# Expert products as plain float32 calls on quarters of the matmul array, in jobs of 96 row slots

## The reference

```python
def moe_swiglu(x, router, w1, w3, w2):
    xt = x.reshape(-1, d)
    logits = (xt @ router).astype(F32)
    top_v, top_i = lax.top_k(logits, TOP_K)          # 2 of 8
    gates = jax.nn.softmax(top_v, axis=-1)
    combine = jnp.sum(jax.nn.one_hot(top_i, N_EXPERTS) * gates[..., None], axis=1)
    for e in range(N_EXPERTS):
        out = out + combine[:, e:e + 1] * swiglu(xt, w1[e], w3[e], w2[e])

def swiglu(x, w1, w3, w2):
    return (jax.nn.silu(x @ w1) * (x @ w3)) @ w2     # 1024 -> 3584 -> 1024
```

## Time and profile before

| | |
|---|---|
| time, median of 3 runs (lowest, highest) | 1520.54 us (1519.48, 1522.57) |
| span of the profiled execution, first to last instruction | 1517.9 us |
| TensorE busy | 1491.3 us, 98% |
| TensorE weight loads busy (beside the products) | 1298.2 us, 86% |
| VectorE, ScalarE busy | 1237.9 us (82%), 962.7 us (63%) |
| bytes read from memory, written | 446.45 MB, 36.87 MB |
| expert stage, first product of the first job to the last product of the last | from 541.95 to about 1503.9 us |

### The profile page before, as it was taken

How to read it: one execution, slowest core, us unless ns; L and a number is a source line. 1 busy time by engine, 2 the same in 40 slices (tenths; PEclk the granted TensorE clock), 3 DMA queues, 4 the chain that set the end, 5 groups by cost and what they waited for, 6 DMA issues and landing times.

```text
span 1517.9 us, 23455 instructions
## 1 busy us (share of the span) xinstructions
PE 1491.3 (98%) x8803; PEld 1298.2 (86%) x8804; DVE 1237.9 (82%) x906; ACT 962.7 (63%) x693; POOL 82.7 (5%) x65
## 2 busy tenths in 40 slices
PE   9998999999999999999999999999999999999997
PEld 9987899999999878888888888888888888888885
DVE  6898865655578788889888888888888888888887
ACT  6634443333353577777777777777777777777774
POOL 1035100000000120000000000000000000000300
PEclk9999999999999999999999999999999999999999
DMA  9644788888555679999999999999999999999991
GB/s 318 214 135 151 268 304 297 298 306 310 188 191 174 225 257 393 395 369 384 373 365 390 368 379 373 369 389 370 374 382 370 373 384 358 387 376 369 387 396 45
DMA packets 212938, 483.97 MB, mean 319 GB/s; under 512 B 8810, under 2 KB 26314, under 8 KB 209820
## 3 DMA queue, kind: packets, MB, share of 16 engines
q1 hardware_dynamic: 209224, 473.67, 85.9%
q10 hardware_dynamic: 2388, 5.32, 0.9%
q0 software_dynamic: 1280, 4.33, 0.7%
HBM read 446.45 MB, written 36.87 MB: 318 GB/s over the span
## 4 chain that ended last, share of the span: by engine, by line
PE 87%; DVE 1%; issue 0%; ACT 0%; DVEq 0%
PE Q L2544 20%; PE Q L2495 14%; PE Q L2497 14%; PE Q L2496 14%; PE Q L2039 7%; PE Q L2040 7%; PE Q L2041 7%; PE Q L2528 2%; DVE wlo L1174 1%; PE Q L2474 0%; PE Q L2505 0%; ACT yrows L1149 0%; PE Q L2400 0%; PE Q L2408 0%; PE Q L2032 0%
## 5 line engine op out<-in xcount | busy, mean ns | idle before, releaser
L1174 DVE TENSOR_TENSOR wlo<-raw,whi 128x2048 fp32r<-128x2048 f32 x413 | 940.6, 2295 | 197.9 <-ACT whi L988 120.1
L988 ACT ACTIVATE whi<-raw 128x2048 fp32r<-128x2048 f32 x336 | 642.9, 1921 | 179.3 <-PE Q L2497 84.1
L2495 PE MATMUL Q<-whi,xgh 128*128 128x512 f32 x896 | 358.0, 400 | 0.0
L2497 PE MATMUL Q<-whi,xgl 128*128 128x512 f32 x896 | 352.9, 394 | 0.0
L2496 PE MATMUL Q<-wlo,xgh 128*128 128x512 f32 x896 | 352.2, 393 | 0.0
L2039 PE MATMUL Q<-xh,whi 128*128 128x264 f32 x1024 | 293.7, 287 | 5.0 <-DVEq L1285 1.8
L2040 PE MATMUL Q<-xl,whi 128*128 128x264 f32 x1024 | 291.2, 284 | 0.0
L2041 PE MATMUL Q<-xh,wlo 128*128 128x264 f32 x1024 | 289.8, 283 | 0.0
L2497 PEld LDWEIGHTS Q<-whi,xgl 128*128 128x128 f32 x896 | 168.7, 188 | 39.3
L2496 PEld LDWEIGHTS Q<-wlo,xgh 128*128 128x128 f32 x896 | 168.7, 188 | 36.5
L2495 PEld LDWEIGHTS Q<-whi,xgh 128*128 128x128 f32 x896 | 168.9, 189 | 35.5
(11 more groups left out here) (286 smaller groups left out, 1140.4 us busy)
## 6 DMA issues: line engine op xcount, KB each, us to landing
raw<-in_moe_w SPq DMA_DIRECT2D x336, 1024.0 KB, 7.6
raw<-in_ffn_w SPq DMA_DIRECT2D x42, 1024.0 KB, 7.5
raw<-in_hgrn_w_in SPq DMA_DIRECT2D x16, 1024.0 KB, 7.3
xg_rows<-zeros SPq DMA_DIRECT2D x6, 2048.0 KB, 10.9
y_rows<-zeros SPq DMA_DIRECT2D x6, 2048.0 KB, 11.5
raw<-in_conv_w_in SPq DMA_DIRECT2D x12, 1024.0 KB, 5.5
raw<-in_hgrn_w_out SPq DMA_DIRECT2D x4, 1024.0 KB, 5.2
raw<-in_conv_w_out SPq DMA_DIRECT2D x4, 1024.0 KB, 5.0
```

The lines of the kernel that those rows point to most:

```text
L988: a.activation(bufs(q)[0], raw[:, n % RAW, PW * (q % 2):PW * (q % 2 + 1)], ACT.Copy).then_inc(hi_done, 1)
L1174: v.tensor_tensor(low, raw[:, slot, PW * half:PW * (half + 1)], high.bitcast(F32), ALU.subtract).then_inc(lo_done, 1)
L2495: t_.matmul(out, xgh[:, kt, :], high[:, w], start=(kt == 0), stop=False)
L2497: mm = t_.matmul(out, xgl[:, kt, :], high[:, w], start=False, stop=(kt == DT - 1))
```

## The change

In the expert stage nothing is split any more. The weights go from memory into a ring of six pieces of 1 MiB (`ring`) and TensorE reads them there; the rows (`xgt`), the turned hidden rows (`ht`) and the weights are plain float32. A job has 96 row slots (`SLOT`), three groups of 32. In `up_m` each slice of the inputs takes six calls with 32 columns of weights: for each group one call over the first 384 of the 512 hidden columns, with its output on that group's own partitions, and then for each group one call over the last 128 columns, all three on partitions 96 to 127. In `down_m` each 128 hidden columns take twelve calls of 256 columns, four at a time on the four quarters of the partitions. A block has 48 + 48 + 48 calls instead of 24 + 24 + 24. `turn` has three transposes. The splits, `hi_m`, `lo_m`, `early`, `hth`/`htl`, `xgh`/`xgl` go away. Five pieces of the first job are loaded during the convolution and one after the routing's last use of that place; every later piece waits until the piece six before it is used. In the last job the result leaves PSUM in five pieces instead of two. The zero fill is 96/128 of its bytes. A few semaphores are merged (`a_mm`, `turned`, `tok_ready`).

```diff
-SPLIT_M = 6
-AHEAD_M = SPLIT_M - 1
+RING = 6
+SLOT = 96
+GROUP = 32
+MAIN = 384
+TAIL = P
+YW = 256
...
-    SLOTS = 3 * P
+    SLOTS = 3 * SLOT
+    GROUPS = SLOT // GROUP
+    PIECES = 2 * JOB
...
+        def y_tail(n):
+            return Q[1][SLOT:P, n // 2, YW * (n % 2):YW * (n % 2 + 1)]
...
+            def load_piece(q, src):
+                slot = q % RING
+                sp.dma_start(ring[:, slot, :].rearrange("p (k w) -> p k w", k=src.shape[1]), src
+                             ).then_inc(piece_loaded[slot], 16)
...
             for c in range(6):
                 chunk(C_CIN + c, kp(conv_w_in[0])[:, :, FW * n:FW * (n + 1)])
+                if c == 3:
+                    sp.wait_ge(sem("squares_summed"), len(NORMS))
+                    for slot in range(4):
+                        sp.wait_ge(sem(f"state_out{slot}"), 16 * SLOT_OF.count(slot))
+                    sp.wait_ge(sem("prompt_state_out"), 32)
+                if c >= 3:
+                    early_piece(c - 3)
             for c in range(2):
                 chunk(C_COUT + c, kp(conv_w_out[0])[:, :, FW * c:FW * (c + 1)])
+                early_piece(3 + c)
+            sp.wait_ge(sem("xs_gained"), TT)
+            sp.wait_ge(sem("xs_ready"), TT)
+            early_piece(5)
+
+            def pair(k, q, src, reg=None):
+                for half in range(2):
+                    free = k * PIECES + (2 * C_MOE + q + half - RING + 1)
+                    sp.wait_ge(used, free if reg is None else free + reg * 6)
+                    n = src.shape[1] // 2
+                    load_piece(q + half, src[:, n * half:n * (half + 1), :])
...
-            early(0)
-            early(1)
-            early(2)
...
-                a.activation(hs[:, :], Q[0][:, 0, :], ACT.Silu).then_inc(sem("hs_ready"), 1)
+                a.activation(hs[:, :], Q[0][:, 0, 0:MAIN], ACT.Silu).then_inc(sem("hs_ready"), 1)
...
-                    for j in range(2):
-                        act.wait_ge(sem("y_mm"), j + 1)
-                        a.activation(yh[:, 512 * j:512 * (j + 1)], Q[1][:, j, :], ACT.Copy
-                                     ).then_inc(sem("yh_ready"), 1)
+                    act.wait_ge(sem("y_mm"), 1)
+                    a.activation(yh[0:SLOT, 0:2 * YW], Q[1][0:SLOT, 0, :], ACT.Copy).then_inc(sem("yh_ready"), 1)
+                    act.wait_ge(sem("y_mm"), 2)
+                    a.activation(yh[0:SLOT, 2 * YW:3 * YW], Q[1][0:SLOT, 1, 0:YW], ACT.Copy)
+                    for n in range(GROUPS):
+                        ins = a.activation(yh[GROUP * n:GROUP * (n + 1), 3 * YW:D], y_tail(n), ACT.Copy)
...
-                        mm = t_.matmul(Q[0][:, 2 + half, P * (d % 4):P * (d % 4 + 1)],
-                                       xs[0:r, t, P * d:P * (d + 1)], pm[0:r, t, :],
+                        mm = t_.matmul(Q[0][:, 2 + half, P * (d % 4):P * (d % 4) + SLOT],
+                                       xs[0:r, t, P * d:P * (d + 1)], pm[0:r, t, 0:SLOT],
...
             def piece(k, q, reg):
-                w = k * (2 * JOB) + (M0 + q + 1)
-                pe.wait_ge(lo_done, w if reg is None else w + reg * 6)
+                n = k * FB + (q // RING + 1)
+                pe.wait_ge(piece_loaded[q % RING], (n if reg is None else n + reg) * 16)
+                return ring[:, q % RING, :]

             def up_m(bank, k, q, reg, first=False):
+                out = Q[0][:, bank, :]
                 for half in range(2):
...
                     for c in range(4):
                         kt = 4 * half + c
-                        w = slice(FW * c, FW * (c + 1))
-                        out = Q[0][:, bank, :]
-                        t_.matmul(out, xgh[:, kt, :], high[:, w], start=(kt == 0), stop=False)
-                        t_.matmul(out, xgh[:, kt, :], low[:, w], start=False, stop=False)
-                        mm = t_.matmul(out, xgl[:, kt, :], high[:, w], start=False,
-                                       stop=(kt == DT - 1))
+                        for n in range(GROUPS):
+                            g_ = slice(GROUP * n, GROUP * (n + 1))
+                            t_.matmul(out[g_, 0:MAIN], xgt[:, kt, g_], w[:, FW * c:FW * c + MAIN],
+                                      start=(kt == 0), stop=(kt == DT - 1), skip_group_check=True)
+                        for n in range(GROUPS):
+                            g_ = slice(GROUP * n, GROUP * (n + 1))
+                            mm = t_.matmul(out[SLOT:P, TAIL * n:TAIL * (n + 1)], xgt[:, kt, g_],
+                                           w[:, FW * c + MAIN:FW * (c + 1)], start=(kt == 0 and n == 0),
+                                           stop=(kt == DT - 1), skip_group_check=True)
                     mm.then_inc(used, 1)
...
-                        for c, j in ([(0, 0), (1, 0), (0, 1), (1, 1)] if by_bank else
-                                     [(0, 0), (0, 1), (1, 0), (1, 1)]):
+                        for cb, c in (itertools.product(range(GROUPS), range(2)) if by_bank else
+                                      [(cb, c) for c in range(2) for cb in range(GROUPS)]):
+                            f = 2 * half + c
+                            bank, col = cb // 2, YW * (cb % 2)
                             for n in range(GROUPS):
+                                mm = t_.matmul(Q[1][GROUP * n:GROUP * (n + 1), bank, col:col + YW],
+                                               rows_of_h(ht, f, n), w[:, D * c + YW * cb:D * c + YW * (cb + 1)],
+                                               start=start, stop=(last and f == 3), skip_group_check=True)
+                            mm = t_.matmul(Q[1][SLOT:P, bank, col:col + YW], rows_of_h(ht, f, cb),
+                                           w[:, D * c + 3 * YW:D * (c + 1)],
+                                           start=start, stop=(last and f == 3), skip_group_check=True)
```

More of the change, by code:

```diff
@@ L11 @@
+import itertools
 from contextlib import ExitStack
@@ L290, in build @@
         raw_loaded = [[sem(f"raw_loaded{i}_{half}") for half in range(2)] for i in range(RAW)]
+        piece_loaded = [sem(f"piece_loaded{i}") for i in range(RING)]
         hi_done, lo_done, used = sem("hi_done"), sem("lo_done"), sem("pieces_used")
@@ L472, in body @@
             def body(k, e, row, ahead):
[L474 to L480, removed]
+                with sp.Fori(0, FB - 2) as i:
+                    pair(k, 6, tiles_of(moe_w3, e, 0, DT)[:, :, bass.ds(i * FW + FW, FW)], i)
+                    pair(k, 8, tiles_of(moe_w2, e, i * 4, 4), i)
+                    pair(k, 10, tiles_of(moe_w1, e, 0, DT)[:, :, bass.ds(i * FW + 2 * FW, FW)], i)
@@ L976, in _ @@
             M0 = 2 * C_MOE
-            def hi_m(k, q0, q1, reg=None):
-                for q in range(q0, q1):
-                    n = q // 2
-                    loads = k * (JOB // RAW) + (n // RAW + C_MOE // RAW + 1)
-                    free = k * (2 * JOB) + (M0 + q - SPLIT_M + 1)
-                    if reg is not None:
-                        loads, free = loads + reg, free + reg * 6
-                    act.wait_ge(raw_loaded[n % RAW][q % 2], loads * 16)
-                    act.wait_ge(used, free)
-                    a.activation(bufs(q)[0], raw[:, n % RAW, PW * (q % 2):PW * (q % 2 + 1)],
-                                 ACT.Copy).then_inc(hi_done, 1)
-            def early(q):
-                if MOE_SLOT[q] < SPLIT:
-                    act.wait_ge(used, M0 + MOE_SLOT[q] - SPLIT + 1)
-                hi_m(0, q, q + 1)
-            early(0)
-            early(1)
-            early(2)
             def row_half(t, j):
@@ L1023, in _ @@
             row_squares(0)
-            early(3)
             act.wait_ge(sem("xt_turned"), 1)
@@ L1862, in _ @@
             M0 = 2 * C_MOE
-            def lo_m(k, q0, q1, reg=None):
-                for q in range(q0, q1):
-                    w = k * (2 * JOB) + (M0 + q + 1)
-                    dve.wait_ge(hi_done, w if reg is None else w + reg * 6)
-                    lo_ins((q // 2) % RAW, q % 2, *bufs(q))
             def mul(nth, last):
@@ L2525, in turn @@
                     pe.wait_ge(sem("hx_ready"), nth + 2)
-                    for c in range(4):
+                    for c in range(GROUPS):
                         mm = t_.transpose(Q[0][:, 2, P * c:P * (c + 1)], hx[:, P * c:P * (c + 1)],
@@ L2530, in turn, with rows_of_h, down_m @@
                     mm.then_inc(sem("h_turned"), 1)
-                def down_m(nth, q, reg, begin, last, ends=False, between=None, hth=hth, htl=htl):
-                    pe.wait_ge(sem("htl_ready"), nth + 1)
+                def rows_of_h(ht, f, n):
+                    return ht[:, f, GROUP * n:GROUP * (n + 1)] if f < GROUPS else ht[:, n, SLOT:P]
+                def down_m(nth, q, reg, begin, last, ends=False, between=None, ht=ht):
+                    pe.wait_ge(sem("ht_ready"), nth + 1)
                     for half in range(2):
-                        piece(k, q + half, reg)
-                        high, low = bufs(q + half)
```

(1 more changed line is left out.)

275 lines of the change are left out of this document (107 added, 168 removed).

## The result

The changed kernel takes 1532.54 us (median; 1530.12 to 1533.37), the kernel before 1520.02 us on the same chip: a ratio of 1.0076, 95% interval 1.0062 to 1.009. The forecast was 1480 us, 40 us less; the change costs 12 us. The profiled execution has a span of 1528.4 us, 4.1 us under the median.

What follows compares the result with a forecast made beforehand. TensorE's stream of calls was taken to set the expert stage (961.9 us). 1517.9 - 49 (stage) + 5 (jumps) + 0.3 (start and end) = 1474; 2.6 to the median gives 1477, 3 for late loads 1480 us; range 1462 to 1526.

Steps and rivals of the forecast that it cites:

- The passes, `up_m`, `down_m`, the block: Expert stage: a pass of N columns takes N x 0.833 + 2.4 ns, `up_m` 5.25 us, `down_m` 5.18, a block 16.2.
- Turning the rows and the two changes of shape: `turn_rows`, once for each of seven jobs: 0.65 us for eight transposes plus 0.2 for shape changes, 0.85 us.
- Quarters at the same time, also of mixed lengths: TensorE calls on different quarters run together; in `up_m` the longer sum, 656 ns a slice, counts.
- late tails: Rival in `up_m`: quarter 3's short calls start late, 760 ns a slice, 17.9 us a block, about 1568 us; chance 0.10.
- strict order: Rival in TensorE's calls: each starts with the second pass of the one before, block 35 us, over 2500 us; chance 0.03.
- The jumps: Job loop of TensorE: each of seven jumps back waits for one program page, 0.7 us each, 5 us in all.
- The upper bound: Jumps back: each waits as long as a 1 MiB load, 7 x 7.6 = 53 us.
- the rival built on it: Rival at the job loop's jumps: they wait long, 1525 us, no change or a little slower; chance 0.06.
- late transfers: Expert stage: 3 us added for TensorE standing before a late load.
- The loads: Expert weights and rows: needing 392 GB/s of 395 shown, just hidden by under 1%; floor 113.5 us a job.
- The rival's 380 GB/s and 118 us: Rival in the expert stage: loads become the bound, 118 us a job, stage 944 us, about 1503 us; chance 0.20.
- Start and end: Outside the expert stage: routing and start 1.5 us less, the last piece's output 1.8 us more, together 0.3 us.

Runs made afterwards that it cites:

- d_loads: Changed kernel with a short job loop and most products left out in the seven looped jobs, every load kept; a job takes 116.05 to 116.17 us.
- d_rows: d_loads with the rows asked for one block earlier; a job takes 116.1 to 117.1 us.
- s_two: Changed kernel with two written blocks instead of four in the job loop, 1,204 instructions instead of 2,374, and next rows asked for a block earlier; 1490.76 us.
- s_best: s_two with the six gathers of earlier jobs' rows held until 37 of the last job's 42 pieces are used; 1490.56 us.

## Why the prediction was wrong, step by step

- **The passes, `up_m`, `down_m`, the block: right.** 16.275 us, forecast 16.2 (4.2 us in 56 blocks). Turning the rows and the two changes of shape: 0.96, forecast 0.85.
- **Quarters at the same time, also of mixed lengths: right.** The rivals "late tails" (17.9 us a block) and "strict order" (35 us) fall with the same number. The Trainium skill, "TensorE: Matmul & The Clock Gate", Part 3, The mechanism, has starts and ends strictly in program order. The trace doesn't agree with that: in one slice the second passes of the long calls start at 700.55 us, after three passes (700.27 to 700.49) of the short calls that stand behind them in the program. The measurement decides.
- **The jumps: the step that failed.** The forecast had 7 x 0.7 = 5 us, the time of the page's own packet in a trace where nobody waited for a page. (The 0.7 comes from a share that is rounded to 0.1%; the 33 packets take 1.04 us each.) There are six jumps, and each costs 44.5 / 6 = 7.4 us: 5.0 us of standing, since the page waits among the weights (2.6 us beside a quarter of them), and 2.4 us at half the clock. The upper bound, 7.6 us as for a load of 1 MiB, was the nearer row, and the rival built on it (1525 us, chance 0.06) is what came, with its sign, a gap once a job at the same line. That 7.6 is so near to 7.4 is luck, since the bound knew nothing of the clock; its 7 x 7.6 = 53 us are even more than the 44.5 measured. The range ended 6 us too low because this rival was put on top of a forecast in which all else holds: blocks, rows and late transfers took 4.2 + 0.8 + 8.3 = 13.3 us more than it counts.
- **The hint that was there.** The Trainium skill, "Runtime: NRT & Kernel Launch", Instruction fetch mechanics, says that a taken branch out of the store stalls for a fetch; its own words are a target outside "the current 2-page window". The stops agree with it, but the window is wider here: by 9.2 pages for 2,374 instructions two pages are some 520, an estimate, and loops of 667 to 1,490 were held. The section's 2,048 instructions for TensorE are more than the runs show to be of use: a loop of 1,649 was already brought anew in each pass. The forecast set the rule beside the sum and gave it a chance of 0.06, though the count, 2,340 (2,374 in fact), spoke for it.
- **The loads: just hidden, it said; just not hidden, it is.** The 1% of room came from 395 GB/s for all of a job's bytes. d_loads and d_rows show 394 for the weights and 386 to 388 for a job. In the changed kernel the stops hid this: TensorE lost 7.4 us a job and the loads caught up in them, so that only 8.3 us of late transfers show (forecast 3). Without the stops a job takes 115.0 us, TensorE's own pace, to 118, where the loads are late. The rival's 380 GB/s and 118 us were the pessimistic end of that.
- **A transfer that the forecast didn't name.** The rows that come back at the start of the last job collide with its loads: 6.8 us in s_two, and 0 in s_best, which holds them back. The 3.9 us at the same place here are put down to the same, without a run of their own. Before, twice as many pieces were buffered and nothing waited.
- **Start and end: right within 1 us.** The first product is 0.6 us earlier (forecast 1.5 with the rest of the routing), from the last product to the end of the span it is 15.3 instead of 14.0 us (forecast 1.8 more).

Sum: 913 + 5 + 3 = 921 us of forecast stage, +4.2 blocks, +0.8 rows, +39.5 jumps, +5.3 late transfers = 971, and 971.8 are measured. With the jumps out of the way, s_two, the time is 1490.8 us: inside the forecast's own 1465 to 1495, though 11 us above its 1480.

## What to carry to other kernels

Count the instructions of a loop before and after a change that makes calls smaller, and keep a loop that runs often well under what the engine holds (here 1,490 was held, 1,649 was not): a jump that leaves it costs 5 us beside full DMA traffic and 1.6 to 2.8 us more at the half clock. Writing the loop out costs no stop, but here 6.4 us more than a loop that is held. Price a fetch by what else stands in the DMA queues at that moment, not by its own packet. And a floor for the loads that is taken from a stretch of pure weights is too low: take it over a whole pass, with everything that comes and goes at its seam.

## What the runs showed of the hardware that was not expected

- A stop of 5 us brings TensorE's granted clock from 1.00 to 0.50 for some 3 us of work, 14.3 us in six jumps; the first wait for `xg`, 1.85 us, did the same and cost some 1.7 more; behind the other one, 0.71 us, the products keep their pace.
- TensorE's loops of 1,649 instructions and more were brought anew in full in each pass, one of 1,490 not at all. Behind a page that TensorE waits for it goes on 1.6 to 1.8 us after the packet's end in the changed kernel, beside 394 GB/s and beside 103 (in the kernel before with a long loop 1.4 to 1.5 us after it).
- A call of 128 columns on one quarter runs beside calls of 384 columns on the three others without loss: 655 ns a slice, the sum of six passes of 109 ns.
